# Two attention layers of a four-layer block: two kinds of heads interleaved, their scores computed in another form

## The reference, cut to what matters

```
a_z, bq, bk, bv, cq, ck, cv = split_proj(h @ w_in[i])      # h: normed and modulated tokens; context the same
out_a: u * (w_s @ rms_norm(v) + b_s), (u, v) = gelu(a_z)   # gated mix over 128 tokens
out_b: 8 heads of 64 rows, 2 key/value heads; softmax over a window of the latent keys,
       the 256 context keys and a sink; scale 64 ** -0.5
out_c: 4 heads, each with two maps of 32 rows:
       pd = softmax(s0) - lam * softmax(s1); out = rms_norm(pd @ v); scale 32 ** -0.5
x = x + g1 * (concat(out_a, out_b, out_c) @ w_out[i]);  x = x + g2 * conv_ffn(...)
```

## Time and profile before

| | |
|---|---|
| three runs | 1733.97 us median (1733.3 to 1743.19) |
| profiled execution | 1732.81 us, span 1731.0 us |
| TensorE, busy | 1612.7 us (93%), 10544 records |
| VectorE, busy | 1101.5 us (64%) |
| ScalarE, busy | 804.8 us (46%) |
| GpSimd, busy | 386.3 us (22%) |
| chain that ended last | TensorE 74%, VectorE 15%, issue 5%, ScalarE 2%, DMA 2% |
| mean granted TensorE clock | 0.972 of 2.4 GHz |

### The profile page before, as it was taken

The page is one execution under the profiler, slowest core; times in us unless marked ns, Lnnn a source line. Parts: engine busy times, 40 slices in busy tenths (PEclk is TensorE's granted clock), DMA queues, the critical chain, the costliest instruction groups (busy, mean ns, idle before and its releaser), DMA issues.

```text
span 1731.0 us, 29754 instructions
## 1 busy us (share of the span) xinstructions
PE 1612.7 (93%) x10544; PEld 1383.0 (80%) x10544; DVE 1101.5 (64%) x1778; ACT 804.8 (46%) x1406; POOL 386.3 (22%) x272
## 2 busy tenths in 40 slices
PE   3999899999999999998979999998989999699997
PEld 1677577588888888695779899796889999489997
DVE  3433964666666477558689985654489854767654
ACT  3423664444444323435545564544545544455543
POOL 0150000000000011056999700020079400000000
PEclk9999999999999999899989999999989999889999
DMA  9555003433322587324136668552557668636653
GB/s 374 214 198 182 25 1 108 139 114 95 97 96 84 176 268 241 105 74 146 40 120 199 198 181 289 185 159 110 188 190 252 216 224 323 246 92 179 184 161 115
DMA packets 76979, 285.13 MB, mean 165 GB/s; under 512 B 8512, under 2 KB 11840, under 8 KB 69216
## 3 DMA queue, kind: packets, MB, share of 16 engines
q1 hardware_dynamic: 58528, 187.34, 33.5%
q0 software_dynamic: 18368, 96.67, 16.0%
HBM read 282.93 MB, written 1.05 MB: 164 GB/s over the span
## 4 chain that ended last, share of the span: by engine, by line
PE 74%; DVE 15%; issue 5%; ACT 2%; DMA 2%; POOL 1%; SPq 0%; DVEq 0%; ACTq 0%
PE B L1543 19%; PE B L1544 19%; PE B L1545 19%; PE B L1741 3%; PE B L1771 3%; DVE WLO L1022 3%; PE B L1564 2%; DVE NORM L1119 2%; DVE HL L1109 2%; PE B L1759 2%; DMA MW<-in_wmod 1%; DVE SM L1179 1%; PE B L1556 1%; PE B L1558 1%; PE B L1557 1%
## 5 line engine op out<-in xcount | busy, mean ns | idle before, releaser
L1543 PE MATMUL B<-HH,WHI 128*128 128x256 f32 (+1 forms) x1872 | 608.0, 325 | 42.6 <-DVE HL L1109 23.0
L1544 PE MATMUL B<-HL,WHI 128*128 128x256 f32 (+1 forms) x1872 | 594.2, 317 | 0.0
L1545 PE MATMUL B<-HH,WLO 128*128 128x256 f32 (+1 forms) x1872 | 594.0, 317 | 0.0
L1022 DVE TENSOR_TENSOR WLO<-RAW,WHI 128x1024 fp32r<-128x1024 f32 (+1 forms) x376 | 451.8, 1205 | 192.1 <-ACT WHI L661 191.5
L661 ACT ACTIVATE WHI<-RAW 128x1024 fp32r<-128x1024 f32 (+1 forms) x376 | 358.9, 959 | 201.5 <-PE B L1545 192.5
L1543 PEld LDWEIGHTS B<-HH,WHI 128*128 128x128 f32 x1872 | 361.8, 193 | 92.8 <-issue 47.3
L1545 PEld LDWEIGHTS B<-HH,WLO 128*128 128x128 f32 x1872 | 362.8, 194 | 22.2
L1544 PEld LDWEIGHTS B<-HL,WHI 128*128 128x128 f32 x1872 | 363.4, 194 | 19.8
L1543 PE MATMUL B<-MIDH,WHI 128*128 128x256 f32 (+1 forms) x704 | 218.3, 310 | 0.0
L1544 PE MATMUL B<-MIDL,WHI 128*128 128x256 f32 (+1 forms) x704 | 217.9, 309 | 0.0
L1545 PE MATMUL B<-MIDH,WLO 128*128 128x256 f32 (+1 forms) x704 | 217.9, 309 | 0.0
(11 more groups left out here) (196 smaller groups left out, 1974.3 us busy)
## 6 DMA issues: line engine op xcount, KB each, us to landing
RAW<-in_wup SPq DMA_DIRECT2D x176, 512.0 KB, 3.9
RAW<-in_wdn SPq DMA_DIRECT2D x64, 384.0 KB, 3.4
WINV<-in_wmod POOLq DMA_DIRECT2D x48, 512.0 KB, 5.0
GWR<-in_wmod POOLq DMA_DIRECT2D x23, 1024.0 KB, 7.6
RAW<-in_wproj SPq DMA_DIRECT2D x44, 512.0 KB, 4.4
RAW<-in_wdn SPq DMA_DIRECT2D x64, 320.0 KB, 3.6
GWA<-in_wmod POOLq DMA_DIRECT2D x15, 1024.0 KB, 5.5
RAW<-in_wout SPq DMA_DIRECT2D x24, 512.0 KB, 4.4
```

The source lines that it names most:

```text
L1022: v.tensor_tensor(WL[s][:, 0:kts, :], RAW[s][:, 0:kts, :], WH[s][:, 0:kts, :].bitcast(F32), ALU.subtract).then_inc(lo_done, 1)
L1543: mm(bank[:, 0:t], wh, a, start=first and k == ks[0], stop=False)
L1544: mm(bank[:, 0:t], wh, b, start=False, stop=False)
L1545: ins = mm(bank[:, 0:t], wl, a, start=False, stop=stop and k == ks[-1])
```

## The change

- The projection's order is gated part, c keys and queries, b, values. The norm of the gated values moves from the attention into the projection (`v_squares`, `v_means`).
- The c scores: of each c query and key tile ScalarE makes an fp32r high part and VectorE the low part. 16 DMAs a tile (`stack`, on SP's queue, between the loads of `w_out`) lay them from SBUF to SBUF into four strips of 32 rows, queries as high, low, high, low and keys as high, high, low, low. One fp32r matmul over 128 rows then gives the full score of one map.
- The b scores: head h of the first 64 rows and head h+4 of the last 64 rows are two fp32 matmuls with 64 rows each, one after the other, into two banks. `KP` and `pads` are gone.
- `slots` alternates c heads and pairs of b heads, for one query tile after the other. There are four score banks in place of three. The mixes back go to the end, with parts of four output blocks between them (`out_part`).
- The queries are negated and scaled by their gains, so a minimum takes the place of the maximum and the small scaling operation behind it. This holds for layer 2 also.

More of the change, by code:

```diff
@@ L364, in items @@
-            u = 0
-            for n, it in enumerate(out):
-                it["n"], it["u"] = n, u
-                u += len(it["maps"])
-            assert u == NUNIT[l] and len(out) == NITEM[l] and grp == NGROUP[l]
-            return out
-        ITEMS = [items(l) for l in range(3)]
+            for qt in range(TT[l] // P):
+                for h in range(8):
+                    val = lambda kt, h=h: SV[:, kt, P * (h // 4):P * (h // 4) + P]
+                    out.append(dict(h=h, qt=qt, keys=(0, 512), q=2 + h, k=h // 4, val=val, grp=grp, n=len(out),
+                                    last=h % 4 == 3, first=h % 4 == 0))
+                    grp += h % 4 == 3
@@ L815, in proj, with copy_pt @@
                         ins.then_inc(bfc, 1)
-            def attention(l):
-                its = ITEMS[l]
-                ub, ib, gbs = total(NUNIT, l), total(NITEM, l), total(NGROUP, l)
-                def exps(it):
-                    for m in range(len(it["maps"])):
-                        u = it["u"] + m
-                        nk = it["keys"][1] - it["keys"][0]
+            def copy_pt(l, i, nk):
+                act.wait_ge(pt_mm, total(NITEM, l) + i + 1)
+                if i >= 2:
+                    act.wait_ge(pv_mm, total(NITEM, l) + i - 1)
+                act_f(PTS[:, i % 2, 0:nk], banks[2 + i % 2][:, 0:nk], ACT.Copy).then_inc(pt_ev, 1)
@@ L825, in exps @@
+            def weave(l):
+                S, nq = SLOTS[l], TT[l] // P
+                ub, ib = total(NUNIT, l), total(NITEM, l)
+                def exps(s):
+                    nk = s["keys"][1] - s["keys"][0]
+                    for m in range(2):
+                        u = s["u"] + m
                         act.wait_ge(nm_done, ub + u + 1)
                         if u >= 4:
-                            first = next(j for j in its if j["u"] <= u - 4 < j["u"] + len(j["maps"]))
-                            act.wait_ge(pt_mm, ib + first["n"] + 1)
@@ L1295, in mix_lo @@
                     ins.then_inc(m_lo, 1)
+                if l == 0:
+                    mod_apply(2, 0)
+                for j in range(len(S) + 4):
+                    if j >= 4 and S[j - 4]["last"]:
+                        group(S[j - 4])
+                    if j < len(S):
+                        minima(S[j])
+                    if 1 <= j <= len(S) and S[j - 1]["kind"] == "c":
+                        combine(S[j - 1])
+                    if j in (1, 2):
+                        gated(j - 1)
+                    if j in (4, 5):
+                        gated_lo(j - 4)
+                    if j == 6:
+                        derive(l, 1)
+                    if j == len(S) + 2:
+                        for k in range(nq - 1):
+                            mix_lo(k)
@@ L1310, in attention @@
[L1310 to L1316 removed]
+                        derive(l, 2)
+                    for k in STEPS[l].get(j - 1, []):
+                        mix_lo(k)
             def residual(l, part, m, bank):
```

497 lines of the change are left out of this document (240 added, 257 removed).

## The result

The changed kernel takes 1727.3 us (median of 14 runs, 1723.7 to 1733.5), the kernel before, beside it, 1735.1: ratio 0.9947, 95% interval 0.993 to 0.9963. It is faster by 0.5%, where 2% were forecast (1699). The profiled execution has a span of 1731.6 us; before it was 1731.0. The profiled execution of the kernel after is the slowest of its 14 (1733.5), that of before (1732.8) lies at the fast end of its own. So the gain doesn't show in the two spans, and stretches have to be compared.

The account below looks back on a forecast made before the run. TensorE was taken to bound pairs with 512 keys (5.3, taken as 5.7 us), VectorE or ScalarE those with 256. Gains of 21.6 (layer 0) + 14.0 (layer 1) - 1.7 = 34 from 1732.8 gave 1699 us, range 1684 to 1718.

Parts of the forecast that it names:

- TensorE's pair, 5.3: Attention, two slots with 512 keys: TensorE needs 0.43 + 1.03 + 1.32 + 2.52 = 5.3 us, and bounds them.
- Row halves overlap: Attention, b scores: two 64-row scores overlap nearly fully on the array, 0.91 us plus 0.12 for two masks.
- A turn costs at most 0.08: Attention: entry to and return from row halves cost at most 0.08 us, 2 us for 24 b slots.
- the rival: Attention: array runs empty at each change between whole and halves, 0.23 at 48 changes, 11 us, 1710; chance 0.05.
- I take 0.4, nearest to the stores: Projection, SP's queue: one stacking DMA's price p taken as 0.4 us, near the stores' 0.33 to 0.45.
- Layer 1 waits 64p - 31: Stacking late, slower than before: layer 1's wait for 64 DMAs at price p; p = 1.2 gives 1769; chance 0.06.
- Layer 0's tiles take about twice as long, so nothing there: Layer 0's projection: ScalarE's copies waiting for stacking lots cost nothing, against about 3 us in layer 1.
- Contention with GpSimd, 1.5 in the attention: Layer 1's attention: eight VectorE combinations can stand behind GpSimd's weighing; 1.5 us taken.
- Given back, 1.7: Layer 1's up-projection: 14 us more of it lie beside GpSimd's weighing, at 12%, costing 1.7 us.
- The chained engines: Attention: three engines chain instead of overlapping, up to 6.9 us per two slots; 24 pairs 1 us more, 1723; chance 0.14.
- the halves in turn: Attention: row halves don't overlap, 16 pairs with 512 keys pay 0.91 more, 15 us, 1714; chance 0.10.
- stacking somewhat late: Projection, SP's queue: stacking DMAs at p 0.5 to 0.8, giving 1702 to 1716; chance 0.10.

Follow-up runs that it names:

- wide: Kernel after with each lot of 16 stacking DMAs made 4 of 128 partitions (stacked tiles then don't hold the right rows); 1711.6 us, ratio 0.9848.
- free_hi: Kernel after with four buffers for the high parts in layer 1, so ScalarE's third and fourth copy don't wait for landings; 1732.9 us, ratio 0.9965.
- whole_b: On wide, the two 64-row scores of a pair each taken over all 128 rows; 1708.8 us, ratio 0.983.
- serial: On wide, all two-map slots of a layer first, then all 64-row slots, the order of before; 1731.4 us, ratio 0.9964.

## Why the prediction was wrong

The forecast's mechanism of the attention held. That its 35.6 us (21.6 and 14.0) stand beside the 35.9 of wide's lead is luck: layer 0 gave 24.4 there and layer 1 11.3, and the 14.0 already had 3 taken off for the stacking. What failed is that term. The prediction put 3 us in its sum for the stacking; the runs give 31.7 (25.5 in layer 1, 6.2 in layer 0, wide against after). The price of one DMA was too low, but this alone wouldn't have put the time out of the range: the waits that it leads to and the work that was to cover it were misjudged too.

- *TensorE's pair, 5.3.* It is 5.74: stacked scores 0.55 for 0.43, halves 1.06 and a mask's 0.12 for 1.03, transposes 1.34 for 1.32, values 2.67 for 2.52. "Taken 5.7" was right for another reason, TensorE being busy all the time and not 93%. With 256 keys it holds the pairs too, at 3.25; 3.7 was taken for the other engines. That is most of why layer 0 from its last projection product took 83.5 us, not 87.8.
- *Row halves overlap:* right. *A turn costs at most 0.08:* too low. Four transposes took 0.54 from start to start before the halves and 0.45 before whole-array scores (whole_b), so entering costs 0.09; before 32-row strips two groups took 0.98 instead of 0.80, 0.18. The halves take 1.06 to the next start where a whole-array score takes 0.97, so leaving costs at most another 0.09. Per 64-row slot that is 0.18 at most, where the rival had 0.46. The Trainium skill (TensorEngine Tiling (Array Packing), Key Properties) says that a change of mode drains the engine; these rows agree with it in sign, at less than half the rival's size.
- *"I take 0.4, nearest to the stores".* This is the first half of the step that failed. The issue took 0.635 us from one to the next. The upper bound, 0.66, was next to it, and the prediction had worked out 11 us for it. With that price its own reckoning gives some 1709, still in the range.
- *"Layer 1 waits 64p - 31".* This is the second half. The terms (3 + 64p + 2, against 35) give 64p - 30, so 10.6 at 0.635; the first score came 17.4 us later than in wide (87.7 against 70.3 behind the 105th split). From bq0's square (737.1) the first issue came after 4.8, not 3: its parts were ready at 737.7, but a load that waited for its buffer stood before it. The issues took 43.1, not 40.6, with the loads between them. The last landing came 4.6 behind the queue's end, not 2. And the cover was 34.2 (wide, 730.9 to 765.1), not 35.2. These differences make up the rest to within about 1. ScalarE's waits, 9.8 and 9.5 where 3 in all were allowed, cost the first score at most 1.7 beside this (free_hi). What is left of the 25.5 is mainly the attention, 67.5 us where wide takes 60.7.
- *"Layer 0's tiles take about twice as long, so nothing there".* ScalarE's copies waited 8.3 and 12.2 us there, and the loss was 6.2 (wide's a against after's). The last lot landed at 172.6, before the last projection product began (175.9), so there the wait at the end is not the cause. That it is the copies' waits is argued; no run takes them out of layer 0 alone. The 64p - 50 of the rival for this layer doesn't follow from tiles of twice the length.
- *Not in the sum: the clock.* The prediction named 0.8 as something that would add to it and priced nothing. Layer 1's attention took 60.7 us at 0.94 (wide) and 67.5 at 0.78 (after).
- *Contention with GpSimd, 1.5 in the attention.* Too small: wide's pairs took 6.7 us on average in layer 1 (775.94 to 816.07 for six) against 5.74, some 6 in all, of which about 1 is the first pair's at half the clock. In three of these pairs TensorE waits for VectorE's combination (L1281); that GpSimd stands behind it is argued. The start, taken as 10, was 13.3 there (last projection product 764.8, first values 778.1). *Given back, 1.7:* 4.4 (d of wide against before). Layer 2's up-projection, counted at nothing, could take 8 more or not.

So of the 35.9 us that the change brings without its many DMAs, these took 25.5 in layer 1 (with the attention's lower clock) and 6.2 in layer 0. The chained engines and the halves in turn are refuted: TensorE has no gap in the pairs of layer 0, and a pair of halves takes 1.13 where the whole array takes 1.88; "stacking somewhat late" was the right case, with a tenth of the chances and at three times the size that its formula gives for 0.635.

What stays open: why the granted clock of one and the same code differs from trace to trace (layer 0's attention: 1.00 in after, 0.94 in free_hi), and with it how much of the 6.8 us by which layer 1's attention is longer than wide's belongs to the stacking. In the profiled execution of the kernel after, 4.2 us more are lost between the 293rd and the 305th split; other kernels lie between 79.5 and 82.1 there, so it is no doing of the change that these runs could show.

## What to carry to other kernels

Count the DMAs a change issues on one queue, and price each by its issue at the upper bound the trace allows: bytes were nearly free here, issues were not, and 64 of them needed more time than the stage that was to hide them. An engine that waits for such a queue to reuse a buffer passes the wait to all that stands behind it in its own order. And where a kernel has stretches with two lengths, compare traces point by point before reading the medians: the row halves' 6.5 us don't show in the medians at all.

## What the runs showed of the hardware

- An SBUF-to-SBUF DMA of 32 partitions and 64 KB and one of 128 partitions and 256 KB took the same 0.6 us to issue on SP's queue. The Trainium skill (DMA: Bandwidth & Descriptors, Bandwidth) calls transfers under 64 KB descriptor-dominated. Most of these DMAs lie at that edge, and the smaller ones (32 KB) and the 256 KB ones took the same time to issue; in the kernel after the count of issues was the price.
- fp32r matmuls on two different 32-row strips overlap: three rounds of two take 0.89 us. Six full-array ones at 0.217 would take 1.30, three 0.65.
- With cheaper scores and no other work between them the two-map slots ran at a granted clock of 0.55, not 1.00 (serial against before, one trace of each), and took 45 us instead of 47.
- A VectorE subtraction of 256 columns took 0.41 us or 2.62 beside the same GpSimd work, by the pattern the two fell into.
